# Loading the feed-forward stage's first operands during the mixing stage

## The reference

```
x  = x + concat(o_a, o_b) @ w_o
h2 = rms_norm(x, ffn_norm)
x  = x + (silu(h2 @ w_gate) * (h2 @ w_up)) @ w_down     # w_gate, w_up: 1024 x 2816
y  = rms_norm(x, final_norm)
```

## Time and profile before

| | us |
|---|---|
| three runs | 4270.46 (median), 4265.92 to 4274.7 |
| the profiled execution | 4274.86 |
| its span, first to last instruction | 4273.1 |
| TensorE busy | 3771.4 (88%) |
| VectorE, ScalarE, GpSimd busy | 2199.8 (51%), 1702.9 (40%), 1376.0 (32%) |
| mean granted TensorE clock | 0.94 of full speed |

### The profile page before, as it was taken

How to read it: one execution, slowest core, us unless ns; L and a number is a source line. 1 busy time by engine, 2 the same in 40 slices (tenths; PEclk the granted TensorE clock), 3 DMA queues, 4 the chain that set the end, 5 groups by cost and what they waited for, 6 DMA issues and landing times. The chain is left out here.

```text
span 4273.1 us, 59472 instructions
## 1 busy us (share of the span) xinstructions
PE 3771.4 (88%) x20612; PEld 2895.5 (68%) x20612; DVE 2199.8 (51%) x4236; ACT 1702.9 (40%) x3219; POOL 1376.0 (32%) x878
## 2 busy tenths in 40 slices
PE   6999976877888888898886689699999999999998
PEld 5777743555555565566663577588788778889986
DVE  4222223699988888889954533244044224305421
ACT  3333322556656666666561322232133223223311
POOL 0000000556555566554001000244343444444332
PEclk9999988789989999999996599899999999999999
DMA  4222222110100000000001145534343433433331
GB/s 168 73 81 89 73 67 55 42 34 26 30 22 20 19 18 10 20 17 11 12 12 42 70 163 191 157 98 126 111 118 98 153 113 88 148 103 106 88 108 56
DMA packets 347845, 324.14 MB, mean 76 GB/s; under 512 B 53088, under 2 KB 285120, under 8 KB 347648
## 3 DMA queue, kind: packets, MB, share of 16 engines
q1 hardware_dynamic: 335520, 277.64, 22.4%
q10 hardware_dynamic: 7344, 26.74, 1.5%
q0 software_dynamic: 4800, 17.43, 1.0%
HBM read 251.57 MB, written 71.43 MB: 76 GB/s over the span
## 5 line engine op out<-in xcount | busy, mean ns | idle before, releaser
L1502 POOL TENSOR_TENSOR ff_w_lo<-ff_stage,ff_w_hi 128x2048 fp32r<-128x2048 f32 (+1 forms) x136 | 610.1, 4486 | 1224.5 <-ACT ff_w_hi L1584 1224.5
L95 PE MATMUL ff_bank<-ff_h_hi,ff_w_hi 128*128 128x512 f32 (+1 forms) x1760 | 618.7, 352 | 29.7 <-DMA ff_h_lo<-scr_h2T 26.1
L96 PE MATMUL ff_bank<-ff_h_lo,ff_w_hi 128*128 128x512 f32 (+1 forms) x1760 | 620.3, 352 | 0.0
L97 PE MATMUL ff_bank<-ff_h_hi,ff_w_lo 128*128 128x512 f32 (+1 forms) x1760 | 618.9, 352 | 0.0
L2176 DVE TENSOR_SCALAR_CACHE_REDUCE at_hit<-at_score,at_su 128x384 bf16<-128x384 f32 (+13 forms) x406 | 599.6, 1477 | 5.3
L1646 DVE TENSOR_TENSOR ff_a_lo<-ff_prod,ff_a_hi 128x512 f32 (+1 forms) x110 | 410.9, 3735 | 170.7 <-ACT ff_a_hi L1598 170.7
L1908 PE MATMUL at_p_t<-at_ident,at_prob 128*128 128x128 f32 x2176 | 332.5, 289 | 134.6 <-ACT at_prob L1988 133.4
L1584 ACT ACTIVATE ff_w_hi<-ff_stage 128x2048 fp32r<-128x2048 f32 (+1 forms) x136 | 252.8, 1859 | 443.0 <-PE ff_bank L97 416.2
L1908 PEld LDWEIGHTS at_p_t<-at_ident,at_prob 128*128 128x128 f32 x2176 | 250.4, 145 | 212.6 <-ACT at_prob L1988 180.5
L1988 ACT ACTIVATE at_prob<-at_prob,at_st 128x1024 f32<-128x1024 f32 (+7 forms) x384 | 342.9, 897 | 123.2 <-DVE at_st L2145 122.9
L95 PEld LDWEIGHTS ff_bank<-ff_h_hi,ff_w_hi 128*128 128x128 f32 x1760 | 331.2, 188 | 79.5 <-issue 31.4
(11 more groups left out here) (267 smaller groups left out, 6611.0 us busy)
## 6 DMA issues: line engine op xcount, KB each, us to landing
ff_stage<-in_w_gate SPq DMA_DIRECT2D x88, 512.0 KB, 4.0
ff_stage<-in_w_up SPq DMA_DIRECT2D x88, 512.0 KB, 5.2
ff_stage<-in_w_down SPq DMA_DIRECT2D x40, 1024.0 KB, 5.2
pj_xt<-in_xT SPq DMA_DIRECT2D x17, 512.0 KB, 3.4
pj_x<-in_x SPq DMA_DIRECT2D x17, 512.0 KB, 4.4
mx_o<-scr_o SPq DMA_DIRECT2D x17, 512.0 KB, 7.1
mx_x<-in_x SPq DMA_DIRECT2D x17, 512.0 KB, 3.4
scr_x<-mx_x ACTq DMA_DIRECT2D x17, 512.0 KB, 8.1
```

Source lines behind the costliest of these rows:

```text
L95: pe.matmul(out, lhs[0], rhs[0], start=start, stop=False)
L96: pe.matmul(out, lhs[0], rhs[1], start=False, stop=False)
L97: return pe.matmul(out, lhs[1], rhs[0], start=False, stop=stop)
L1502: pool.tensor_tensor(w_lo[a][:, 0:w], stage[a][:, 0:w], w_hi[a][:, 0:w].bitcast(F32), ALU.subtract).then_inc(s_wlo, 1)
```

## The change

A new class `FfnHead` holds the buffers for the first group's rows, both staging buffers, the first of two pairs of weight parts, and five semaphores. It is made before `mix_out` and lives through both stages, with a clearing and a barrier of its own at the very end. POOL, in `mix_out`, issues the loads: the rows of tile t as soon as their stores have landed (t = 0 to 3), unit 0 of the weights after tile 4's rows are stored, unit 1 after tile 6's. ACT makes the high part of unit 0 behind its loop, between `norm(15)` and `take_h(15)`, and POOL then its low part. In `ffn` these loads and this split are left out; ACT splits unit 1 at its start and SP begins with g_final and unit 2. `ht`, a buffer that nothing used, is gone.

```
 mix_out, gpsimd:
-            pass
+            for t in range(4):
+                pool.wait_ge(s_sh, 32 * (t + 2))
+                head.load_h(pool, scr, t, t, P, head.s_h)
+            for a in range(2):
+                pool.wait_ge(s_sh, 32 * (6 + 2 * a))
+                head.load_gate_up(pool, io, a, 0, head.s_w[a])
+            pool.wait_ge(head.s_whi, 1)
+            pool.tensor_tensor(head.w_lo[:, :], head.stage[0][:, :], head.w_hi[:, :].bitcast(F32), ALU.subtract).then_inc(head.s_wlo, 1)
 mix_out, scalar, after the loop:
+            act.wait_ge(head.s_w[0], 32)
+            act.activation(head.w_hi[:, :], head.stage[0][:, :], ACT.Copy).then_inc(head.s_whi, 1)
             take_h(T - 2)
             norm(T - 1)
 ffn, sync:
-                if gr.g == 0:
-                    load_gate_up(gr, 0, 0)
-                    load_h(gr)
-                    load_gate_up(gr, 1, 0)
-                else:
+                if gr.g:
                     for a in range(2):
                         free(gr.unit0 + a)
-                        load_gate_up(gr, a, 0)
+                        head.load_gate_up(sp, io, a, 0, s_wt[a])
 ffn, gpsimd:
-            low(0, 0, 2 * D)
             low(1, 1, 2 * D)
 ffn, tensor:
-                pe.wait_ge(s_h, 32 * (gr.y0 + len(gr.tiles)))
-                if gr.g:
+                if gr.g == 0:
+                    pe.wait_ge(head.s_h, 32 * 4)
+                else:
+                    pe.wait_ge(s_h, 32 * (gr.y0 + len(gr.tiles) - 4))
                     pe.wait_ge(s_y, 2 * gr.y0 - 4)
 ffn, scalar:
-            high(groups[0], 0)
-            high(groups[0], 1)
+            act.wait_ge(head.s_w[1], 32)
+            act.activation(w_hi[1][:, :], stage[1][:, :], ACT.Copy).then_inc(s_whi, 1)
 new:
+class FfnHead:
+    def load_h(self, eng, scr, i, t, n, sem):
+        for a, dst in enumerate((self.h_hi, self.h_lo)):
+            src = scr["h2T"][t, :, a, :].rearrange("p (k t) -> p k t", k=KD)
+            eng.dma_start(dst[:, :, i * P:i * P + n].bitcast(F32), src[:, :, 0:n]).then_inc(sem, 16)
+    def load_gate_up(self, eng, io, a, q, sem):
+        for n, w in enumerate(("w_gate", "w_up")):
+            src = io[w].rearrange("(k p) f -> p k f", p=P)[:, :, ds(q * 2 * P + a * P, P)]
+            dst = self.stage[a][:, n * D:(n + 1) * D].rearrange("p (k f) -> p k f", k=KD)
+            eng.dma_start(dst, src).then_inc(sem, 16)
 build:
+    with ExitStack() as ctx:
+        head = FfnHead(Mem(nc, ctx, "fh"))
+        mix_out(nc, io, scr, head)
+        ffn(nc, io, scr, head)
```

More of the change, by code:

```diff
@@ L1185, in _, with mix_out @@
             run(dve, attended, prologue)
-def mix_out(nc, io, scr):
+def mix_out(nc, io, scr, head):
     with ExitStack() as ctx:
@@ L1198, in mix_out @@
         ht_hi, ht_lo = m.sb("ht_hi", [P, D], F32R), m.sb("ht_lo", [P, D], F32R)
-        ht = m.sb("ht", [P, D])
         squares, st = m.sb("squares", [P, D], BF16), m.sb("st", [P, 8])
@@ L1404, in _, with ffn @@
             split_h(T - 1)
-def ffn(nc, io, scr):
+def ffn(nc, io, scr, head):
     groups = [FfnGroup(g) for g in range(FG)]
@@ L1413, in ffn @@
         m = Mem(nc, ctx, "ff")
-        h_hi, h_lo = m.sb("h_hi", [P, KD, NMAX], F32R), m.sb("h_lo", [P, KD, NMAX], F32R)
+        h_hi, h_lo, stage = head.h_hi, head.h_lo, head.stage
         a_hi, a_lo = m.sb("a_hi", [P, FB, NMAX], F32R), m.sb("a_lo", [P, FB, NMAX], F32R)
-        stage = [m.sb(f"stage{a}", [P, 2 * D]) for a in range(2)]
-        w_hi = [m.sb(f"w_hi{a}", [P, 2 * D], F32R) for a in range(2)]
-        w_lo = [m.sb(f"w_lo{a}", [P, 2 * D], F32R) for a in range(2)]
+        w_hi, w_lo = [head.w_hi, m.sb("w_hi1", [P, 2 * D], F32R)], [head.w_lo, m.sb("w_lo1", [P, 2 * D], F32R)]
         g_final = m.sb("g_final", [P, D])
@@ L1426, in ffn @@
         s_wt = [m.sem(f"w{a}_in") for a in range(2)]
-        s_whi, s_wlo = m.sem("w_hi_done"), m.sem("w_lo_done")
+        s_whi, s_wlo = head.s_whi, head.s_wlo
         s_gu, s_gate, s_prod = m.sem("gate_up_products"), m.sem("gate_done"), m.sem("prod_done")
@@ L1435, in loaded @@
         def loaded(gr, u):
-            a = u % 2
+            a, before = u % 2, gr.g * (FB * 16 + DOWN * 16) - 32
             if u < FB:
-                return s_wt[a], gr.g * (FB * 16 + DOWN * 16) + 32 * (u // 2 + 1)
-            return s_wt[a], gr.g * (FB * 16 + DOWN * 16) + FB * 16 + 16 * ((u - FB) // 2 + 1)
+                return s_wt[a], before + 32 * (u // 2 + 1)
+            return s_wt[a], before + FB * 16 + 16 * ((u - FB) // 2 + 1)
         def width(u):
@@ L1456, in load_h @@
             def load_h(gr):
-                if gr.g:
-                    sp.wait_ge(*used(groups[gr.g - 1], FB - 1))
+                sp.wait_ge(*used(groups[gr.g - 1], FB - 1))
                 for i, t in enumerate(gr.tiles):
[L1460 to L1469, removed]
+                    head.load_h(sp, scr, i, t, gr.rows(i), s_h)
             def free(u):
@@ L1487, in _ @@
                         free(gr.unit0 + a + 2 * q)
-                        load_gate_up(gr, a, q)
+                        head.load_gate_up(sp, io, a, q, s_wt[a])
                 for j in range(2 * DOWN):
@@ L1668, in _, with __init__ @@
                     dve.scalar_tensor_tensor(x1[0:r, i, :], x1[0:r, i, :], rstd[0:r, i:i + 1], g_final[0:r, :], ALU.mult, ALU.mult).then_inc(s_out, 1)
+class FfnHead:
+    def __init__(self, m):
+        N = FfnGroup(FG - 1).N
+        self.h_hi, self.h_lo = m.sb("h_hi", [P, KD, N], F32R), m.sb("h_lo", [P, KD, N], F32R)
+        self.stage = [m.sb(f"stage{a}", [P, 2 * D]) for a in range(2)]
+        self.w_hi, self.w_lo = m.sb("w_hi", [P, 2 * D], F32R), m.sb("w_lo", [P, 2 * D], F32R)
+        self.s_h = m.sem("h_in")
+        self.s_w = [m.sem(f"w{a}_in") for a in range(2)]
+        self.s_whi, self.s_wlo = m.sem("w_hi_done"), m.sem("w_lo_done")
+    def load_h(self, eng, scr, i, t, n, sem):
[7 more added lines that the diff above has]
+            eng.dma_start(dst, src).then_inc(sem, 16)
 class FfnGroup:
@@ L2321, in build @@
         attend(nc, io, scr, kv, [TileClass(LAST, 1, (TK - TP) * P)], min(TOPK, (PAST + NEW) // 4), "as")
-    mix_out(nc, io, scr)
-    ffn(nc, io, scr)
+    with ExitStack() as ctx:
+        head = FfnHead(Mem(nc, ctx, "fh"))
+        mix_out(nc, io, scr, head)
+        ffn(nc, io, scr, head)
 def rope_tables(dim):
```

## The result

| | before | changed |
|---|---|---|
| median of 8 runs each, us | 4270.36 | 4250.96 |
| lowest and highest | 4265.92, 4277.37 | 4241.81, 4258.41 |
| profiled execution | 4274.86 | 4255.5 |
| its span | 4273.1 | 4253.4 |

The changed kernel is faster: ratio 0.995, 95% interval 0.9942 to 0.9959, or 19.4 us by the medians. Forecast were 16.45 us.

What follows compares the result with a forecast made beforehand. PE was taken as the bound, held at the feed-forward's start by the transfer of 4 MB of rows. 4274.86 - 19.05 + 2 + 0.6 = 4258.4, so -16.45 us, or 4254.0 from the median; range 4247 to 4264.

Steps and rivals of the forecast that it cites:

- The wait at the boundary: Feed-forward's start: PE's first matmul moves from 2724.95 to 2705.9, a gain of 19.05 us (17.05 to 19.35).
- the gap stays: After the barrier: something else the wait covered still holds PE, 12 us of it left, 4266; chance 0.05.
- What is late next: Feed-forward: unit 1 ready at about 2712 for a need at 2719.4, unit 2 in the old order; cost nothing.
- ACT's copy and POOL's subtraction: Mixing stage's end: 1.91 us on ACT and 4.49 us on POOL, both under cover; cost 0.
- The collisions: Mixing loop: POOL's six 1 MB loads may delay the x1 store; 2 us taken between 0 and 6.
- Doubled cost of small pieces: Mixing stage: POOL's pieces cost DMA engines twice 3.2 us; chance 0.15 for 4258 to 4262, 0.07 for 4262 to 4272.
- POOL's issue: Mixing stage: each of twelve loads takes POOL 4.2 us to issue, 51 us in all, hidden.
- The slower rival: POOL's list ends after the mixing stage; at 21 us an issue 4288 us; chance 0.05.
- The extra clearing: Kernel's end: one more clearing and barrier cost 0.6 us (0.3 to 1.0).
- The slow start: Feed-forward's first matmuls: PE's 0.43 us a matmul against 0.23 later was taken to stand before and after alike.

Runs made afterwards that it cites:

- rows only: Changed kernel, but units 0 and 1 of the weights loaded by SP and split in the feed-forward, only the rows loaded in the mixing stage; 4264.9 us, ratio 0.9984.
- in the burst: Changed kernel with each of POOL's six 1 MB loads held back until the next turn's row stores are about to be issued; 4255.8 us, ratio 0.9956.
- reload: Changed kernel with POOL's row loads repeated 18 times more, each once the last landed, weight units issued right behind tile 3's rows; 4268.0 us, ratio 0.9984.
- SP's queue: Changed kernel with the same twelve loads issued by SP instead of POOL, behind waits for the stores; 4351.0 us, ratio 1.0183.

## Why the prediction was right

**The wait at the boundary** was the whole effect: 19.7 us from release to matmul became 0.5 in the traces, where the forecast took 2705.9 - 2705.28 = 0.6. The 17.05 to 19.35 of its gain held the 19.2 measured, near the upper end. Nothing else that the wait had covered held PE behind it; the rival "the gap stays" is out.

**What is late next** held: no two starts of the changed kernel's matmuls from 2705.28 on lie more than 1.7 us apart, and none in unit 0's and unit 1's products more than 0.6, so units 1 and 2 were in time. (Before, unit 2 was SP's fourteenth and fifteenth issue, not its twelfth, as the prediction had it; nothing hangs on it.) That it matters showed in *rows only*, where unit 0 became the wait.

**ACT's copy and POOL's subtraction** cost nothing (stage 270.9 us without, 271.0 with).

**The collisions** are the term that was mis-sized: 2 us forecast, nothing measured (stage 271.0 against 271.2 before). The 2 was a choice between bounds of 0 and 6, which held both cases; with 0 the total would have been 1 us off instead of 3, with 6 it would have been 7. Three assumptions were off. POOL's loads were taken to land 7 to 9 us after their issue as in the earlier trace rows, and landed after 4.0 to 6.0; the issue was taken as 4.2 us, which would have put the second load of a pair at the end of the gap of 5.5 us or behind it, and took 0.88; and a load that shares a burst was given up to 1.0 us where *in the burst* measured 0.6 on average. With the first two, the loads are done when the x1 store of the next burst is issued: unit 1's second load landed at 2578.64, and that store was issued at 2578.90.

**Doubled cost of small pieces.** The page speaks against this rival: the twelve loads took q1 down by 12480 packets, 1040 apiece, and q0 up by only 1728, 144 apiece, yet the shares moved by 0.5% of the span on both, some 21 us of 16 engines for 6 MB or 3.5 us for 1 MB, near the 3.2 of the forecast. The shares are rounded; by the durations of all packets in the two traces it is 20.4 us more on q0 and 22.6 us less on q1, 3.4 and 3.8 us for 1 MB, where the rival needed 6.4. (Its 8 to 10 us in all do not follow from its own terms either: with half of the 6.4 us in the gap, 3.2 - 2.2 = 1.0 us a load makes 6.) POOL's queue makes fewer packets of the same pieces, in the same time.

**POOL's issue** was taken as 4.2 us between 0.53 and 4.2, and measured 0.88. The Trainium skill, "DMA: Bandwidth & Descriptors", section "Anatomy of one DMA — SWDGE (gpsimd) path", which let many descriptors pass before their number is felt, came nearer: eight times the pieces cost 0.35 us more. The slower rival needed 19.6 us an issue and was out by this; its mechanism is real, though, as *reload* showed by landing times instead of issues.

**The extra clearing** cost 0.4 us within the span (0.6 forecast): the start of the last matmul is followed by 19.1 us to the end of the span instead of 18.7. Outside the span the profiled execution takes 2.1 us instead of 1.8, in all profiles of changed versions; whether that belongs to the clearing is not shown. **The slow start** was not quite the same, 0.4 us shorter: the granted clock was 0.50 for the first 3.6 us of the feed-forward's matmuls instead of 4.7.

Sum by the traces: -19.2 (wait) - 0.2 (stage) - 0.4 (slow start) + 0.4 (clearing) = -19.4 from the start of the mixing stage to the end of the span. The stage began 0.3 us earlier (the spans differ by 19.7), and 0.3 us more pass outside the span, which leaves 4255.5 - 4274.86 = -19.4.

## What to carry to other kernels

A stage's first loads can be moved into the stage ahead if a queue with an empty list is there to wait for their inputs; the same loads in a queue that serves that stage's loop, ahead of what its next turn needs, cost 16 us a turn. Of several waits that end together, each taken away alone shows little: count what is late next before judging a part. Loads released by the landing of a burst's stores fell in the gap behind it at no price; held back into the next burst they cost 0.6 us each. And loads must stay clear of the last stores before a barrier, as one that went out beside them moved it by 4.6 us.

## What the runs showed of the hardware

- PE's granted clock stayed at 1.00 (2.4 GHz) over gaps of 2.37 us and 1.98 us before the feed-forward; behind one of 2.87 us PE went on at 0.50 (1.2 GHz) for 3 us. The loop's gaps of 1.5 us left it at 1.00 from 2463 to 2678 in the changed kernel. But one gap of 2.69 us, ahead of tile 16's products, was followed within 1.1 us by 3.4 us at 0.50 in 11 of the 13 profiles that have it, and in the other two (*reload*, *SP's queue*) by none. So the length of a gap alone does not tell. A window of the kernel before, behind that gap (2674.8 to 2677.5):

```profile
2678.60:2681.80 3.20, 3.20 (x9) 2.52 (x8) 0.61 (x3) 1.35 (x3) 0.00 (x0) 0.50 0.93 348
```
- POOL issues a load of 1024 pieces in 0.88 us (1.16 the first time) and one of 128 rows in 0.53; the first makes 144 packets there and 1040 from SP's queue, for about the same time of the DMA engines (3.4 and 3.8 us for 1 MB).
- With one pair of POOL loads (1 MB) in flight beside full bursts of the other queues, the loop lost 0.1 us a turn in *reload* and 0.6 in *in the burst*, and POOL's loads took up to 10.5 and 11.2 us to land; with up to six loads in flight it lost up to 4.3 us in a turn.
